# Two mixer layers: the steps of sparse attention go in pairs, at every second turn of the chunk recurrence

## The reference, cut to what matters

```python
def step(S, inp):                       # rwkv7, one token
    r_t, w_t, k_t, v_t, a_t, b_t = inp
    sa = jnp.einsum('bhvk,bhk->bhv', S, a_t)
    S = S * w_t[:, :, None, :] + sa[..., None] * b_t[:, :, None, :] + v_t[..., None] * k_t[:, :, None, :]
    return S, jnp.einsum('bhvk,bhk->bhv', S, r_t)
...
# dsa_mixer, one block of 128 queries; idx are the topk keys
logits = jnp.einsum('bqhc,bqkc->bqhk', q_lat_b, c_sel)
prob = jax.nn.softmax(jnp.where(valid[:, :, None, :], logits, -jnp.inf), axis=-1)
o_lat = jnp.einsum('bqhk,bqkc->bqhc', prob, c_sel)
return jnp.einsum('bqhc,hcd->bqhd', o_lat, w_uv)
```

## Time and profile before

| | |
|---|---|
| median of 3 runs | 3828.14 us (3824.9 to 3833.9) |
| the profiled execution | 3832.01 us, its span 3829.9 us |
| granted TensorE clock, mean | 0.984 |
| PE busy | 3680.9 us, 96% of the span |
| DVE, ACT, POOL busy | 2487.2, 1967.2, 402.6 us |
| chunks with sparse attention, layer 0 | 2265.2 to about 2318 us |
| chunks with sparse attention, layer 1 | 3350.9 to about 3403.6 us |

### The profile page before, as it was taken

One profiled execution on the slowest core, in us unless ns is written; L12 is line 12 of the kernel. 1 busy time (PEld: TensorE's weight loads), 2 busy tenths in 40 slices (PEclk: granted clock), 3 DMA queues, 4 the chain that ended last, 5 costly groups with the idle time before them and its releaser, 6 DMA issues.

```text
span 3829.9 us, 58308 instructions
## 1 busy us (share of the span) xinstructions
PE 3680.9 (96%) x24282; PEld 3052.6 (80%) x24282; DVE 2487.2 (65%) x4181; ACT 1967.2 (51%) x3277; POOL 402.6 (11%) x327
## 2 busy tenths in 40 slices
PE   7999999999989999999999998999999999899998
PEld 5767888878868888888888577888888887678887
DVE  4387699985375999964456856544544568655445
ACT  3466688874465888842344544332423355443323
POOL 0132101130021001310001200000000011000000
PEclk9999999999999999999999899999999999899999
DMA  6573699982203999932222001222222221012222
GB/s 253 190 287 135 246 428 427 427 338 88 88 3 129 422 427 426 407 117 110 96 90 96 23 25 67 103 95 99 105 92 107 94 100 50 3 61 95 100 99 72
DMA packets 61840, 633.53 MB, mean 165 GB/s; under 512 B 6487, under 2 KB 6743, under 8 KB 26888
## 3 DMA queue, kind: packets, MB, share of 16 engines
q1 hardware_dynamic: 46888, 576.32, 37.9%
q0 software_dynamic: 8640, 31.46, 2.1%
q10 hardware_dynamic: 6048, 22.02, 1.4%
HBM read 601.43 MB, written 33.60 MB: 166 GB/s over the span
## 4 chain that ended last, share of the span: by engine, by line
PE 72%; DVE 18%; ACT 6%; issue 2%; DMA 2%; POOL 1%; SPq 0%; POOLq 0%; DVEq 0%; ACTq 0%
PE ps L396 14%; PE ps L401 13%; PE ps L400 13%; DVE arena_r L1532 3%; DVE wbuf_r L377 2%; PE ps L1666 2%; PE ps L1688 2%; PE ps L1686 2%; PE ps L1687 2%; PE ps L1668 2%; PE ps L1667 2%; DVE wbuf_r L1532 1%; ACT arena_r L1525 1%; DVE hT_r L2052 1%; PE ps L446 1%
## 5 line engine op out<-in xcount | busy, mean ns | idle before, releaser
L377 DVE TENSOR_TENSOR wbuf_r<-slot,wbuf_r 128x512 fp32r<-128x512 f32 (+2 forms) x824 | 585.0, 725 | 679.2 <-ACT wbuf_r L367 678.7
L400 PE MATMUL ps<-arena_r,wbuf_r 128*128 128x512 f32 x2688 | 1019.9, 379 | 0.0
L367 ACT ACTIVATE wbuf_r<-slot 128x512 fp32r<-128x512 f32 (+2 forms) x824 | 496.5, 611 | 603.3 <-PE ps L401 527.4
L396 PE MATMUL ps<-hT_r,wbuf_r 128*128 128x512 f32 x2016 | 773.7, 384 | 6.6 <-DVE arena_r L779 4.6
L401 PE MATMUL ps<-hT_r,wbuf_r 128*128 128x512 f32 x2016 | 765.3, 380 | 1.1 <-issue 1.1
L400 PEld LDWEIGHTS ps<-arena_r,wbuf_r 128*128 128x128 f32 x2688 | 508.9, 189 | 72.5 <-issue 2.6
L396 PEld LDWEIGHTS ps<-hT_r,wbuf_r 128*128 128x128 f32 x2016 | 381.8, 189 | 73.2 <-DVE arena_r L779 5.8
L401 PEld LDWEIGHTS ps<-hT_r,wbuf_r 128*128 128x128 f32 x2016 | 381.6, 189 | 55.8 <-issue 1.5
L396 PE MATMUL ps<-arena_r,wbuf_r 128*128 128x512 f32 x704 | 270.6, 384 | 3.3 <-DVE arena_r L2998 2.4
L401 PE MATMUL ps<-arena_r,wbuf_r 128*128 128x512 f32 x672 | 254.7, 379 | 0.0
L1532 DVE TENSOR_TENSOR arena_r<-arena,arena_r 128x1024 fp32r<-128x1024 f32 x164 | 195.3, 1217 | 26.6 <-ACT arena_r L1525 26.6
(11 more groups left out here) (609 smaller groups left out, 7167.2 us busy)
## 6 DMA issues: line engine op xcount, KB each, us to landing
arena<-in_moe SPq DMA_DIRECT2D x82, 2048.0 KB, 20.5
slot<-in_moe SPq DMA_DIRECT2D x56, 2048.0 KB, 20.6
slot<-in_gu SPq DMA_DIRECT2D x40, 2048.0 KB, 7.6
slot<-in_ada SPq DMA_DIRECT2D x20, 2048.0 KB, 7.9
slot<-in_down SPq DMA_DIRECT2D x16, 2048.0 KB, 7.7
slot<-in_win SPq DMA_DIRECT2D x12, 2048.0 KB, 7.5
yrow<-arena ACTq DMA_DIRECT2D x42, 512.0 KB, 11.2
slot<-in_hgrn SPq DMA_DIRECT2D x8, 2048.0 KB, 7.8
```

What stands on the lines that cost most here:

```text
L367: a.activation(hi[:, 0:w], src[:, off:off + w], ACT.Copy).then_inc(*act.mark(c.name, "hi", i))
L377: v.tensor_tensor(lo[:, 0:w], src[:, off:off + w], hi[:, 0:w].bitcast(F32), ALU.subtract) \
L396: p.matmul(bank, hi[:, cs], by_halves(rh[:, k, :]), start=k == 0, stop=False, skip_group_check=True)
L400: p.matmul(bank, hi[:, cs], by_halves(rl[:, k, :]), start=False, stop=False, skip_group_check=True)
```

## The change

`weave` in the stretch of the chunks gets sparse attention through a new generator, `by_twos`, on all three engines. Its first turn does nothing, its second does two steps one directly behind the other, its third nothing, and so on. No instruction is added or taken away on any engine; those of sparse attention in the two stretches change places with those of the chunks.

```diff
+        def by_twos(work):
+
+            while True:
+                yield
+                if next(work, True) or next(work, True):
+                    return
+                yield
+
...
             edge(pe, m.name + " chunks")
-            weave(chunks_pe(p, m), dsa)
+            weave(chunks_pe(p, m), by_twos(dsa))
             mix_out_pe(p, m)
...
-            weave(chunks_act(a, m), dsa)
+            weave(chunks_act(a, m), by_twos(dsa))
...
-            weave(chunks_dve(v, m), dsa)
+            weave(chunks_dve(v, m), by_twos(dsa))
```

## The result

The changed kernel takes 3847.01 us (median of 5 runs, 3845.51 to 3848.63) against 3828.14 us: 18.9 us more, a ratio of 1.0047 with a 95% interval from 1.0034 to 1.0060. Its profiled execution took 3847.07 us with a span of 3845.3.

What follows compares the result with a forecast made beforehand. TensorE was taken to bound both stretches; gaps 7.2, pairs 1.5, tail 0.4 and closing 0.85, less 0.7 of old waits, gave 9.2 us a stretch, +18.5 us for two, a median of about 3847 us; range 3837 to 3860.

Steps and rivals of the forecast that it cites:

- TensorE sets the pace, and a step hides each link: Both stretches: TensorE bounds them; one sparse attention step between two recurrence links outlasts the way through the other engine.
- The price of a gap: Recurrence links with no step between: four S to W at 0.91, three U to S 0.65, three W to U 0.53; 7.2 us.
- The tail: Work that wide pairs leave on ScalarE and VectorE delays the next link, as U's copy behind W of chunk 3: 0.4 us.
- the walk: Step-by-step timing of the pair with 384 and 512 keys, from the start of its scores, using the earlier trace.
- The rival that it lands five times in full: ScalarE's whole 1.2 us backlog delays the next link behind each of five wide pairs: 6.0 us a stretch, 3860; chance 0.06.
- The inside of a pair: Five wide pairs: the next head's values wait for ScalarE's copy of the previous sum, 0.3 us each, 1.5 a stretch.
- The closing: Closing of heads 4 and 5: W of chunk 7 no longer stands in between, so TensorE waits 0.85 us.
- What goes against it: Part of TensorE's 1.45 us of waits a stretch goes, as narrow units' transposes stand behind another unit's work: 0.7 us saved.
- Nothing gives it back: Behind each stretch the recurrence's outputs and the rest of the mixer hang on its end, so the loss is not recovered.
- The clock: Granted clock in the two stretches: forecast to stay at 1.00 (2.4 GHz).
- the rival in which it falls: Short waits drop the granted clock to 0.83 in the stretches, 10 us more each, time 3867 us; chance 0.06.
- TensorE has slack: Both stretches: up to 13.4 us each might be slack, so the time would stay 3828 us; chance 0.06.

Runs made afterwards that it cites:

- The kernels with one kind of bare gap: Changed kernel with seven pairs of steps a stretch instead of eleven, leaving only W to U or only S to W without a step: 3837.06 and 3843.29 us.
- in the odd turns: Changed kernel with the pairs of sparse attention steps moved from the even turns to the odd ones: 3847.88 us, ratio 1.0048.
- the second bank: Changed kernel with two PSUM banks for the heads' sums instead of one, the recurrence rotating through three instead of four: 3845.70 us, ratio 1.0046.
- The recurrence alone: Changed kernel with no sparse attention step beside the recurrence; the 22 steps follow behind its outputs: 3880.21 us, ratio 1.0137.

## Why the prediction was right, and where it was not

- **TensorE sets the pace, and a step hides each link.** Right. The kernels with one kind of bare gap show it best: 3.2 and 6.6 us a stretch for seven gaps each, with the same work, the same number of pairs and the same clock.
- **The price of a gap.** Forecast 0.91, 0.65 and 0.53 us for S to W, U to S and W to U; from start to start 0.85, 0.65 and 0.43. For the gaps behind VectorE I had added a hand-over of 0.12 from another wait; here it is about 0.06. And the gap into chunk 1, which I had priced like the others from S to W, is 0.53, with VectorE's one instruction. Ten gaps and ScalarE's tail together were to cost 7.2 + 0.4; they cost 6.8 in layer 0.
- **The tail.** It falls where the walk put it, on U's copy behind the pair of chunk 3, and makes that gap 1.10 instead of 0.65: 0.45 against the 0.4 in the sum. The rival that it lands five times in full is out.
- **The inside of a pair.** The waits are there and about as long as forecast, but the term came out at half. The next head's values start 0.40 to 0.55 us after the last transposes of a wide pair, which occupy 0.22: five waits of 0.18 to 0.33, 1.4 us against the 1.5 in the sum (matmul rows reach past the point at which the next can start, so that only three show there, with 0.17). Yet each of the five pairs takes only 0.06 to 0.23 us more than its two steps took apart in the kernel before, 0.7 in all. In the walk two errors met. In the pair behind W of chunk 3 the copy of the sum started 2.39 us after the pair's first scores (2288.85 to 2291.24, rows below), where the walk had 2.73: it had taken each step of ScalarE's and VectorE's from the earlier trace rows one after the other, while here the copy started 0.16 after the transposes' copy (2291.08), whose row alone is 0.26 long. And TensorE was there sooner than the walk had it too: its transposes, begun at 2291.46, were through by about 2.8, not 3.0 to 3.2.

```profile
2288.85 0.91 PE L3621 MATMUL ps<-arena,wbuf 128*128 128x384 f32 x2
...
2291.08 0.26 ACT L3691 ACTIVATE arena<-ps 128x128 f32<-128x128 f32 x1
2291.24 0.59 ACT L3699 ACTIVATE slot<-ps 128x512 f32<-128x512 f32 x1
2291.46 0.38 PE L3634 MATMUL ps<-const,arena 128*128 128x128 f32 x2
2291.87 0.49 PE L3646 MATMUL ps<-arena 128*128 128x128 f32 x2
```

- **The closing.** Right: 0.86 from start to start (2321.72 to 2324.06, less 0.49 for W and 0.99 for the values), against 0.85. The row's 0.69 leaves out what the rows before it overlap.
- **What goes against it.** Mis-sized: 0.7 of the 1.45 us of waits was to go. The two pairs with the narrow units, behind W of chunk 1 and behind U of chunk 6, take 0.74 and 0.61 us less than their steps did apart, 1.35 in all, and the closing's old wait, 0.36, has gone into its 0.86. With this and the 0.7 the eleven pairs together take 0.1 us less than the 22 steps apart: what the waiting costs, 6.7, is the bare gaps and the tail.
- **Nothing gives it back.** Right: 1031.3 and 1031.6 us between the stretches.
- **The clock.** I forecast 1.00 and gave the rival in which it falls 0.06, for a whole stretch. It fell in part: one piece at 1.2 GHz in the middle of each stretch, 1.3 and 1.4 us, which goes when the gaps are filled, and one at the start of layer 1, 1.6 us, which the gaps didn't make. The window of the outputs, on which I had set the rival aside, was no guide to it. The Trainium skill, TensorE: Matmul & The Clock Gate, A second HAM failure mode, says that frequent short idling between groups of matmuls makes the clock swing. The pieces in the middle agree with it; the four stretches with seven bare gaps of one kind, and layer 0's with eleven in the odd turns, kept 1.00.
- **TensorE has slack.** Wrong as a rival. By the Trainium skill, Perfetto Trace Analysis, Identifying the Most-Contended Engine, a weight-load share of 74% would leave room. This case's traces don't agree: the stretch with W to U bare, at a clock of 1.00, had none that could have taken in the 3.2 us.

So the mechanism was right, and that the number was met so closely (18.9 us measured, 18.5 forecast) is in good part luck. Against the sum of 9.2 us a stretch the waiting cost 6.7: 0.8 less in the gaps, 0.8 in the wide pairs, 0.65 in the narrow ones and 0.35 in the closing's old wait. The clock, which the sum did not have, brought 2.7 us for both stretches where the gaps were bare, and 1.6 more at the start of layer 1 in the execution that was profiled.

## What to carry to other kernels

Beside a recurrence whose links go through another engine, a step of independent work in every gap is worth the whole way through that engine; two in every other gap leave the other gap bare, and the doubled one gave next to nothing back here (0.1 us a stretch). The price of a bare gap can be read beforehand from a trace in which it is hidden: from the start of the producer to the end of the other engine's work, and a hand-over (about 0.05 us here), less what the producer occupies. If a gap must be bare, choose the cheapest (here W to U, half of S to W).

## What was not expected of the hardware

- Ten waits of 0.4 to 1.3 us in 62 us went with a piece at 1.2 GHz in the middle of the stretch, at nearly the same place in five of five stretches with these pairs (the two of the changed kernel, one with pairs in layer 0 alone, two with the second bank). Each came right behind the longest wait, that for U of chunk 3 (1.0 us, with the second bank 1.3). In none of the six stretches with useless matmuls in the gaps was there one in the middle, and the best of these kernels was faster by 4 to 5 us than the changed one (3842.8 against 3847.0; 13.9 and 18.9 over their own runs of before). Whether the one long wait matters or the sum of them, the runs don't tell.
- The recurrence alone ran at a granted clock of 0.52 although TensorE was busy in 28.5 of 39.6 us by its rows, which are longer at that clock.
- A float32 matmul of 128 by 128 columns occupied TensorE 0.255 us, a transpose of the same size 0.11.
